# Rotary queries of latent attention: products formed from an SBUF copy made by ScalarE instead of from PSUM

## The chip, the cores and the metric

One Trainium2 chip, one core. The metric is the device time of one execution in microseconds. The five engines of the core run instruction streams of their own and meet at semaphores: TensorE (PE in the rows; PEld is its weight load), VectorE (DVE), ScalarE (ACT), GpSimd (POOL) and SyncE (SP), which issues most of the DMA.

## The reference, cut to what matters

Two decoder layers, one with multi-head latent attention (16 heads) and one with sliding-window attention, for a prompt of 1024 tokens and 8 sample tokens. The change is in the first. For every head:

```
q = einsum('bsc,chd->bshd', cq, w_qb)
q_nope, q_rope = q[..., :QK_NOPE], q[..., QK_NOPE:]
rot = concatenate([-xf[..., half:], xf[..., :half]])
q_rope = xf * cos + rot * sin
sc = (einsum(q_nope, k_nope) + einsum(q_rope, kpe)) * MLA_SCALE
o  = softmax(masked sc) @ v
```

The rotary part of a query has 64 rows, so two heads share one tile of 128 partitions.

## The kernel before, in words

The program has a phase that projects the inputs, a phase with the 16 heads (about 300 to 935 us of the span), and later phases that the diff does not touch. The heads phase is `mla_heads`. It is written out by hand: `tensor`, `vector`, `scalar`, `gpsimd` and `sync` each list, for an even and for an odd head, the order of their steps, and a step waits on semaphores for its inputs and its buffers. An engine never passes a step that waits.

Steps of TensorE. `job(kind, x, c)` projects keys (`k`, line 886, two jobs a head), queries (`qn`, line 880, three jobs of 344 columns), values (`v`, line 893) or the rotary queries of two heads (`qr`, line 880, three jobs in an even head: column chunks 2, 0 and 1, in this order). `score(h, t)` (lines 910 to 916) makes the scores of query tile t, `turn` (line 930) transposes probabilities, `mix` (line 946) multiplies them with the values. After the first twelve jobs all jobs use PSUM bank 7, one after the other: a job waits in `bank_read` until the job before it has been read. For a `qr` job this is `qr_mul`, five products.

The rotary chain of one `qr` job: `rope_products` on VectorE forms one product with the cosines over 128 partitions (line 769) and four with the sines over 32 partitions each (line 772), all from PSUM into `rot`; `rope_sum` (line 778) adds them; `high` on ScalarE rounds them into `qr` for each of the two heads (line 671); `rope_low` on VectorE writes the remainders (line 788) and raises `qr_lo`. `rot` has one buffer. `score(h, t)` waits for `qr_lo` of the column chunks that hold its tile: chunk 2 for tiles 6 and 7, chunk 0 for tiles 0 and 1, chunk 1 for tiles 3 to 5.

Other steps named below: `greatest` (line 797, VectorE, maximum of a tile's scores), `exponents` (line 698, ScalarE, waits for that maximum), `invert` (line 806), `norm` (line 607, GpSimd), `turned_high` and `turned_low` (lines 707 and 811), `apply_gate` (line 822), `low` of a k or qn job (lines 751 and 746), `cut` (lines 618 and 620, GpSimd, then two DMA issues) and `split` (lines 597 and 599, GpSimd, weights into a high and a low part).

The order around the third rotary job, in `even(h)` of TensorE and of VectorE:

```
job("qr", p, 1), mix(h, 1, 0), mix(h, 1, 1), job("k", h + 2, 0), score(h + 1, 1)      # then odd: turn, turn, score(h + 1, 4)
rope_products(p, 1), apply_gate(h, 1), rope_sum(p, 1), rope_low(p, 1), low("k", h + 2, 0)
```

Of the kernel before, what the change touches and what calls it, by code (L numbers as in the profile page):

```python
# [18 lines left out]
P = 128  # L19
# [5 lines left out]
CH = TOK // 3  # L25
# [17 lines left out]
ACT = mybir.ActivationFunctionType  # L43
ALU = mybir.AluOpType
# [403 lines left out]
def head_jobs():  # L448

    jobs = [("k", 0, 0), ("k", 0, 1), ("qn", 0, 2), ("qr", -1, 2), ("qn", 0, 0), ("qr", -1, 0), ("qn", 0, 1), ("qr", -1, 1)]  # L450
    jobs += [("v", 0, c) for c in range(4)]
    first = len(jobs)
    for h in range(H - 1):
        if h % 2 == 0:
            p = h // 2
            jobs += [j for j in (("k", h + 1, 0), ("k", h + 1, 1), ("qn", h + 1, 2), ("qr", p, 2), ("qr", p, 0),
                                 ("qn", h + 1, 0), ("qn", h + 1, 1), ("qr", p, 1), ("k", h + 2, 0)) if j[0] != "k" or j[1] < H]
        else:
            p = (h + 1) // 2
            jobs += [("k", h + 1, 1), ("qn", h + 1, 2), ("v", p, 0), ("qn", h + 1, 0), ("v", p, 1), ("v", p, 2),  # L460
                     ("qn", h + 1, 1), ("v", p, 3)]
    return jobs, first


JOBS, N_FIRST = head_jobs()
JOB_NO = {j: n for n, j in enumerate(JOBS)}
# [3 lines left out]
TURNED_NO = {j: n for n, j in enumerate(TURNED)}  # L470
# [19 lines left out]
def turned_heads(p):  # L490

    return [(e, 2 * p + 1 + e) for e in range(2) if 0 <= 2 * p + 1 + e < H]


def job_bank(n):

    return 7 - n % 4 if n < N_FIRST else 7
# [9 lines left out]
def mla_heads(nc, a, g, st):  # L507


    ps = g.ps  # L510
    def sb(name, shape, dt=F32):
        return st.enter_context(nc.sbuf_tensor(name, shape, dt))

    def sem(name):
        return st.enter_context(nc.semaphore(name))
# [4 lines left out]
    vh, vl = sb("b_vh", [P, 3, SEQ], R32), sb("b_vl", [P, 3, SEQ], R32)  # L520
    qh, ql = sb("b_qh", [P, 2, TOK], R32), sb("b_ql", [P, 2, TOK], R32)
    qr = sb("b_qr", [P, 3, TOK], R32)
    rot = sb("b_rot", [P, 2, CH])
    gate = sb("b_gate", [P, 4, 2 * P])
    prob = sb("b_prob", [P, 4, SEQ])
    pth, ptl = sb("b_pth", [P, 4, 512], R32), sb("b_ptl", [P, 4, 512], R32)
# [6 lines left out]
    w_rounded, w_split = sem("b_w_rounded"), sem("b_w_split")  # L533
    gate_in = [sem(f"b_gate_in{u}") for u in range(4)]
    pj_done, pj_hi, pj_lo = sem("b_pj_done"), sem("b_pj_hi"), sem("b_pj_lo")
    qr_mul, qr_rot, qr_hi, qr_lo, kept = sem("b_qr_mul"), sem("b_qr_rot"), sem("b_qr_hi"), sem("b_qr_lo"), g.qs_rope_kept
    scored, maxed, exped, inverted, normed = (sem("b_scored"), sem("b_maxed"), sem("b_exped"),
                                              sem("b_inverted"), sem("b_normed"))
    turned, pt_hi, pt_lo = sem("b_turned"), sem("b_pt_hi"), sem("b_pt_lo")
# [117 lines left out]
    def scalar(act):  # L657
        act.wait_ge(mask_in, 16)
        nc.scalar.activation(maskr[:], mask[:], ACT.Copy).then_inc(mask_ok, 1)

        def high(kind, x, c):

            if (kind, x, c) not in JOB_NO:
                return
            n = JOB_NO[(kind, x, c)]
            bank, cols = job_bank(n), slice(c * CH, (c + 1) * CH)
            if kind == "qr":
                act.wait_ge(qr_rot, TURNED_NO[(kind, x, c)] + 1)
                for e, h in turned_heads(x):
                    rows = qr_rows(e)[0]  # L670
                    nc.scalar.activation(qr[rows, h % 3, cols], rot[rows, 0, :], ACT.Copy, scale=MLA_SCALE).then_inc(qr_hi, 1)
                    if c == 2:
                        nc.scalar.activation(g.qs_rope[:, h, :], rot[rows, 0, CH - DEC:CH], ACT.Copy,
                                             scale=MLA_SCALE).then_inc(kept, 1)
                return
            act.wait_ge(pj_done, n + 1)
            if kind == "qn":
                if c == 2:
                    nc.scalar.activation(g.qs_nope[:, x, :], ps[:, bank, CH - DEC:CH], ACT.Copy,
                                         scale=MLA_SCALE).then_inc(g.qs_kept, 1)  # L680
                nc.scalar.activation(qh[:, x % 2, cols], ps[:, bank, 0:CH], ACT.Copy, scale=MLA_SCALE).then_inc(pj_hi, 1)
            elif kind == "k":
                nc.scalar.activation(kh[:, x % 2, c * 512:(c + 1) * 512], ps[:, bank, :], ACT.Copy).then_inc(pj_hi, 1)
            else:
                for i, (heads, slots) in enumerate(v_slots(x)):
                    copy = nc.scalar.activation(v_view(vh, slots, c), v_psum(bank, heads), ACT.Copy)
                copy.then_inc(pj_hi, 1)

        def exponents(h, t):
            if h >= H:  # L690
                return
            n, keys = tile_no(h, t), (t + 1) * P
            act.wait_ge(maxed, n + 1)
            if n >= 4:
                last = (h, t) if t is None else divmod(n - 4, NT)
                m = TILE_ORDER[last[1]] // 2
                act.wait_ge(turned, chunk_no(last[0], m, m) + 1)
            nc.scalar.activation(prob[:, n % 4, 0:keys],  # L698
                                 ps[:, 2 * (n % 2):2 * (n % 2) + 2, :].rearrange("p b n -> p (b n)")[:, 0:keys],
                                 ACT.Exp, bias=least[:, n % 4:n % 4 + 1], accum_out=total[:, n % 4:n % 4 + 1]).then_inc(exped, 1)  # L700

        def turned_high(h, m, c):
            n, cols = chunk_no(h, m, c), 512 if c < m else 384
            act.wait_ge(turned, n + 1)
            if due(n - 3):
                act.wait_ge(mixed, n - 3)
            nc.scalar.activation(pth[:, n % 4, 0:cols], ps[:, 4 + n % 2, 0:cols], ACT.Copy).then_inc(pt_hi, 1)  # L707

        def even(h):
            p = h // 2  # L710
            turned_high(h, 3, 0), turned_high(h, 3, 1), exponents(h, 1)
            high("k", h + 1, 0), turned_high(h, 3, 2), high("k", h + 1, 1)
            exponents(h, 4), exponents(h, 5)
            high("qn", h + 1, 2), turned_high(h, 3, 3), turned_high(h, 0, 0), turned_high(h, 2, 0)
            high("qr", p, 2), exponents(h, 2), exponents(h, 3)
            turned_high(h, 2, 1), turned_high(h, 2, 2)
            high("qr", p, 0), high("qn", h + 1, 0)
            exponents(h + 1, 6), turned_high(h, 1, 0), exponents(h + 1, 7)
            high("qn", h + 1, 1), turned_high(h, 1, 1), exponents(h + 1, 0)
            high("qr", p, 1), high("k", h + 2, 0)  # L720

        def odd(h):
            p = (h + 1) // 2
            turned_high(h, 3, 0), turned_high(h, 3, 1), exponents(h, 1)
            high("k", h + 1, 1), turned_high(h, 3, 2), high("qn", h + 1, 2), turned_high(h, 3, 3)
            exponents(h, 4), exponents(h, 5)
            high("v", p, 0), turned_high(h, 0, 0), exponents(h, 2), high("qn", h + 1, 0)
            turned_high(h, 2, 0), turned_high(h, 2, 1), high("v", p, 1), exponents(h, 3), high("v", p, 2)
            turned_high(h, 2, 2), exponents(h + 1, 6), turned_high(h, 1, 0), exponents(h + 1, 7)
            high("qn", h + 1, 1), turned_high(h, 1, 1), exponents(h + 1, 0), high("v", p, 3)  # L730

        for j in JOBS[:N_FIRST]:
            high(*j)
        exponents(0, 6), exponents(0, 7), exponents(0, 0)
        for h in range(0, H, 2):
            even(h), odd(h + 1)

    def vector(dve):
# [20 lines left out]
        def rope_products(p, c):  # L759
            if ("qr", p, c) not in JOB_NO:  # L760
                return
            n, k = JOB_NO[("qr", p, c)], TURNED_NO[("qr", p, c)]
            bank, cols = job_bank(n), slice(c * CH, (c + 1) * CH)
            dve.wait_ge(pj_done, n + 1)
            if k:
                dve.wait_ge(qr_hi, qr_halves[k - 1])
                dve.wait_ge(qr_lo, qr_halves[k - 1])
                dve.wait_ge(kept, sum(len(turned_heads(j[1])) for j in TURNED[:k] if j[2] == 2))
            nc.vector.tensor_tensor(rot[:, 0, :], ps[:, bank, 0:CH], g.cos[:, cols], ALU.mult).then_inc(qr_mul, 1)
            for r in range(4):  # L770
                to, src = slice(32 * r, 32 * r + 32), slice(32 * (r ^ 1), 32 * (r ^ 1) + 32)
                nc.vector.tensor_tensor(rot[to, 1, :], ps[src, bank, 0:CH], g.sin[src, cols], ALU.mult).then_inc(qr_mul, 1)

        def rope_sum(p, c):
            if ("qr", p, c) not in JOB_NO:
# [81 lines left out]
    def tensor(pe):  # L857
        def bank_read(n):

            if JOBS[n] in PLAIN_NO:  # L860
                pe.wait_ge(pj_lo, PLAIN_NO[JOBS[n]] + 1)
            else:
                pe.wait_ge(qr_mul, 5 * (TURNED_NO[JOBS[n]] + 1))

        def job(kind, x, c):

# [124 lines left out]
    p = Programs(sync, gpsimd, scalar, vector, tensor)  # L991
# [1724 lines left out]
```

## Time and profile before

| | |
|---|---|
| median of 3 runs | 1764.34 us (1761.11 to 1766.4) |
| profiled execution, its own time | 1767.28 us |
| its span | 1765.6 us |
| mean granted clock of TensorE | 0.961 |
| busy: TensorE, weight loads | 1630.6 us (92%), 1524.4 us (86%) |
| busy: VectorE, ScalarE, GpSimd | 827.7 us (47%), 545.1 us (31%), 740.0 us (42%) |

Shares are of the whole span. The view of waits adds up, for a waiting line, the idle time that one releasing line ended. The timelines give each instruction's start from the beginning of the span, its duration and, in brackets, the idle time of its engine before it where there was some. An "xN" merges N instructions in a row. "Issue" is an idle time for which the view found no releaser.

### The profile page before, as it was taken

The page shows a single profiled execution, that of the slowest core. Times are in us where ns is not written, and L with a number is a line of the kernel's source. Part 1 is how long each engine was busy: PE and PEld are TensorE (multiplying, and loading weights), DVE is VectorE, ACT ScalarE, POOL GpSimd, SP SyncE. Part 2 cuts the span into 40 slices and gives each one's busy share as a digit, 9 for nine tenths or more (in the row PEclk, how much of TensorE's full clock was granted, in tenths as well). Part 3 has the DMA queues.
Part 4 walks back from the last instruction along what each step waited for, and adds up shares of the span by engine and source line. Part 5 has one row for each costly group of instructions (what it writes and reads, how often), then busy time and mean ns, then how long its engine had stood idle before and what let it go on. Part 6 is the DMA issues. An engine that isn't in the chain of part 4 may idle for free. (4 is left out here: it accounts for less than half of the span.)

```text
span 1765.6 us, 28128 instructions
## 1 busy us (share of the span) xinstructions
PE 1630.6 (92%) x10778; PEld 1524.4 (86%) x10778; DVE 827.7 (47%) x1471; ACT 545.1 (31%) x1201; POOL 740.0 (42%) x894
## 2 busy tenths in 40 slices
PE   6999997899999999999997879998999999799797
PEld 6989997799999999998985569997899999576797
DVE  5127311576675756757563320029644210687016
ACT  5022111344444444444432210012322301575012
POOL 2323332255554555555445204546324222487410
PEclk9999998999999999999999998998999999799698
DMA  4112231111221112112149882252453212542214
GB/s 170 60 48 95 95 113 61 39 61 51 64 67 52 58 61 65 56 56 72 37 147 303 302 307 77 69 199 100 144 191 131 67 72 107 166 116 67 85 45 160
DMA packets 101406, 186.92 MB, mean 106 GB/s; under 512 B 11058, under 2 KB 65091, under 8 KB 100995
## 3 DMA queue, kind: packets, MB, share of 16 engines
q1 hardware_dynamic: 86628, 139.36, 23.7%
q0 software_dynamic: 8448, 24.65, 4.0%
q10 hardware_dynamic: 6208, 21.26, 3.0%
q8 instruction: 78, 1.28, 0.3%
q14 instruction: 44, 0.36, 0.1%
HBM read 137.42 MB, written 49.89 MB: 106 GB/s over the span
## 5 line engine op out<-in xcount | busy, mean ns | idle before, releaser
L607 POOL TENSOR_SCALAR b_prob<-b_prob,b_share 128x896 f32<-128x896 f32 (+7 forms) x128 | 97.1, 759 | 198.5 <-DVE b_share L806 196.7
L1649 POOL CAST w_hi_d<-w_raw_d 128x1024 fp32r<-128x1024 f32 x38 | 40.4, 1064 | 233.4 <-PE ps L129 128.5
L129 PE MATMUL ps<-a_xh,w_hi_a 128*128 128x344 f32 x552 | 119.6, 325 | 13.7 <-DVE a_xl L280 10.4
L707 ACT ACTIVATE b_pth<-ps 128x512 fp32r<-128x512 f32 (+1 forms) x160 | 86.2, 555 | 104.3 <-PE ps L930 94.7
L129 PE MATMUL ps<-a_xl,w_hi_a 128*128 128x344 f32 x552 | 118.1, 323 | 0.0
L129 PE MATMUL ps<-a_xh,w_lo_a 128*128 128x344 f32 x552 | 117.4, 321 | 0.0
L797 DVE TENSOR_REDUCE b_least<-ps 128x1 f32<-128x896 f32 (+7 forms) x128 | 96.3, 752 | 35.8 <-PE ps L916 35.1
L698 ACT ACTIVATE b_prob<-ps,b_least 128x896 f32<-128x896 f32 (+7 forms) x128 | 94.8, 743 | 57.3 <-DVE b_least L797 56.3
L811 DVE TENSOR_TENSOR b_ptl<-ps,b_pth 128x512 fp32r<-128x512 f32 (+1 forms) x160 | 99.2, 632 | 27.1 <-ACT b_pth L707 26.1
L129 PEld LDWEIGHTS ps<-a_xh,w_hi_a 128*128 128x128 f32 x552 | 93.8, 190 | 15.0 <-issue 10.8
L107 POOL CAST w_hi_a<-w_raw_a 128x1024 fp32r<-128x1024 f32 x23 | 24.9, 1082 | 181.6 <-PE ps L129 177.0
L880 PE MATMUL ps<-cqh,b_w_hi 128*128 128x344 f32 x300 | 99.2, 331 | 0.2 <-DVE b_ql L746 0.2
L880 PE MATMUL ps<-cql,b_w_hi 128*128 128x344 f32 x300 | 96.1, 320 | 0.0
L880 PE MATMUL ps<-cqh,b_w_lo 128*128 128x344 f32 x300 | 95.9, 320 | 0.0
L946 PE MATMUL ps<-b_pth,b_vh 128*128 128x256 f32 x320 | 93.1, 291 | 2.5 <-DVE b_ov L822 2.5
L129 PEld LDWEIGHTS ps<-a_xl,w_hi_a 128*128 128x128 f32 x552 | 94.5, 191 | 0.0
L930 PE MATMUL ps<-ident,b_prob 128*128 128x128 f32 x576 | 87.7, 278 | 5.7 <-POOL b_prob L607 5.5
L129 PEld LDWEIGHTS ps<-a_xh,w_lo_a 128*128 128x128 f32 x552 | 92.8, 189 | 0.0
L946 PE MATMUL ps<-b_pth,b_vl 128*128 128x256 f32 x320 | 90.1, 282 | 0.0
L946 PE MATMUL ps<-b_ptl,b_vh 128*128 128x256 f32 x320 | 89.9, 281 | 0.0
L1652 POOL TENSOR_TENSOR w_lo_d<-w_raw_d,w_hi_d 128x1024 fp32r<-128x1024 f32 x35 | 88.6, 2531 | 2.8
L1928 PE MATMUL ps<-xo_h,w_hi_d 128*128 128x344 f32 x304 | 81.9, 330 | 5.7 <-DVE w_lo_d L1800 3.6
(348 smaller groups left out, 4690.0 us busy)
## 6 DMA issues: line engine op xcount, KB each, us to landing
w_raw_d<-in_w_tiles SPq DMA_DIRECT2D x46, 512.0 KB, 3.6
c_pages<-in_cache_pages SPq DMA_DIRECT2D x80, 160.0 KB, 4.5
w_raw_a<-in_w_tiles SPq DMA_DIRECT2D x23, 512.0 KB, 3.5
gate_scratch<-a_stage ACTq DMA_DIRECT2D x16, 512.0 KB, 2.6
b_gate<-gate_scratch SPq DMA_DIRECT2D x64, 128.0 KB, 2.6
oh_scratch<-b_oh POOLq DMA_DIRECT2D x64, 128.0 KB, 2.1
ol_scratch<-b_ol POOLq DMA_DIRECT2D x64, 128.0 KB, 2.1
xo_h<-oh_scratch SPq DMA_DIRECT2D x16, 512.0 KB, 10.1
```

The lines of the kernel that those rows point to most:

```text
L129: mm = nc.tensor.matmul(ps[:, bank + c, 0:CH], wt, xt[:, k0 + k, c * CH:(c + 1) * CH], start=first and x == 0, stop=last and x == 2)
L607: nc.gpsimd.tensor_scalar(prob[:, n % 4, 0:keys], prob[:, n % 4, 0:keys], share[:, n % 4:n % 4 + 1], 1.0, ALU.mult, ALU.mult).then_inc(nor ...
L698: nc.scalar.activation(prob[:, n % 4, 0:keys], ps[:, 2 * (n % 2):2 * (n % 2) + 2, :].rearrange("p b n -> p (b n)")[:, 0:keys], ACT.Exp, bi ...
L707: nc.scalar.activation(pth[:, n % 4, 0:cols], ps[:, 4 + n % 2, 0:cols], ACT.Copy).then_inc(pt_hi, 1)
L797: nc.vector.tensor_reduce(least[:, n % 4:n % 4 + 1], ps[:, 2 * (n % 2):2 * (n % 2) + 2, :].rearrange("p b n -> p (b n)")[:, 0:keys], AX.X, ...
L811: nc.vector.tensor_tensor(ptl[:, n % 4, 0:cols], ps[:, 4 + n % 2, 0:cols], pth[:, n % 4, 0:cols].bitcast(F32), ALU.subtract).then_inc(pt_l ...
L880: mm = nc.tensor.matmul(ps[:, bank, 0:CH], wt[:, own], xt[:, k, c * CH:(c + 1) * CH], start=k == 0 and i == 0, stop=k == 3 and i == 2)
L930: mm = nc.tensor.transpose(ps[:, 4 + n % 2, col:col + P], prob[:, (first + q) % 4, (2 * c + b) * P:(2 * c + b + 1) * P], g.ident[:])
L946: mm = nc.tensor.matmul(ps[:, 6, 2 * P - wide:2 * P], vt[:, h % 3, v], pt[:, n % 4, col:col + wide], start=c == 0 and k == 0 and i == 0, s ...
L1649: nc.gpsimd.tensor_copy(hi, shaped(raw_tile(t), t)).then_inc(w.rounded, 1)
L1652: nc.gpsimd.tensor_tensor(lo, shaped(raw_tile(t), t), hi.bitcast(F32), ALU.subtract).then_inc(w.split, 1)
L1928: mm = nc.tensor.matmul(ps[:, bank + i, 0:CH], wt, xt[:, half * KT + k, c * CH:(c + 1) * CH], start=half == 0 and k == 0 and x == 0, stop= ...
```

## The change

ScalarE copies the bank of a `qr` job into a third slot of `rot` and raises `qr_raw`. The five products wait for that and read the copy. The bank is given to the next job when the copy is made. The copy waits until the products of the rotary job before it are done. In `even(h)` of ScalarE the copies stand at three places written by hand; in the first jobs each stands right before its `high`.

```diff
-    rot = sb("b_rot", [P, 2, CH])
+    rot = sb("b_rot", [P, 3, CH])
...
+        def raw_of(kind, p, c):
+            if (kind, p, c) not in JOB_NO:
+                return
+            n, k = JOB_NO[("qr", p, c)], TURNED_NO[("qr", p, c)]
+            act.wait_ge(pj_done, n + 1)
+            if k:
+                act.wait_ge(qr_mul, 5 * k)
+            nc.scalar.activation(rot[:, 2, :], ps[:, job_bank(n), 0:CH], ACT.Copy).then_inc(qr_raw, 1)
...
-            high("qn", h + 1, 2), turned_high(h, 3, 3), turned_high(h, 0, 0), turned_high(h, 2, 0)
-            high("qr", p, 2), exponents(h, 2), exponents(h, 3)
+            high("qn", h + 1, 2), turned_high(h, 3, 3), turned_high(h, 0, 0), raw_of("qr", p, 2), turned_high(h, 2, 0)
+            high("qr", p, 2), exponents(h, 2), exponents(h, 3), raw_of("qr", p, 0)
             turned_high(h, 2, 1), turned_high(h, 2, 2)
...
-            high("qr", p, 1), high("k", h + 2, 0)
+            raw_of("qr", p, 1), high("qr", p, 1), high("k", h + 2, 0)
...
         for j in JOBS[:N_FIRST]:
+            if j[0] == "qr":
+                raw_of(*j)
             high(*j)
...
-            dve.wait_ge(pj_done, n + 1)
+            dve.wait_ge(qr_raw, k + 1)
...
-            nc.vector.tensor_tensor(rot[:, 0, :], ps[:, bank, 0:CH], g.cos[:, cols], ALU.mult).then_inc(qr_mul, 1)
+            nc.vector.tensor_tensor(rot[:, 0, :], rot[:, 2, :], g.cos[:, cols], ALU.mult).then_inc(qr_mul, 1)
             for r in range(4):
                 to, src = slice(32 * r, 32 * r + 32), slice(32 * (r ^ 1), 32 * (r ^ 1) + 32)
-                nc.vector.tensor_tensor(rot[to, 1, :], ps[src, bank, 0:CH], g.sin[src, cols], ALU.mult).then_inc(qr_mul, 1)
+                nc.vector.tensor_tensor(rot[to, 1, :], rot[src, 2, :], g.sin[src, cols], ALU.mult).then_inc(qr_mul, 1)
...
-                pe.wait_ge(qr_mul, 5 * (TURNED_NO[JOBS[n]] + 1))
+                pe.wait_ge(qr_raw, TURNED_NO[JOBS[n]] + 1)
```

## Rows read from the trace of the kernel before

**Rows 1.** TensorE's waits, heads stage: line, releaser, us in total, times, longest.

```profile
PE ps L886 <- DVE b_rot L772: 10.7, 7, 1.5
...
PE ps L910 <- DVE b_vl L755: 2.8, 1, 2.8
PE ps L910 <- issue: 2.2, 1, 2.2
```

**Rows 2.** Timeline of TensorE around T in head 2: start, us, what, [idle before].

```profile
452.77 0.47 PE L886 MATMUL ps<-ckvh,b_w_hi 128*128 128x512 f32 x1 [1.52 <-DVE b_rot L772]
...
455.74 0.47 PE L910 MATMUL ps<-b_kh,b_qh 128*128 128x512 f32 x1
...
457.60 0.45 PE L886 MATMUL ps<-ckvh,b_w_hi 128*128 128x512 f32 x1
```

**Rows 3.** Timelines of VectorE, ScalarE and GpSimd at the same place.

```profile
449.94 0.52 DVE L769 TENSOR_TENSOR b_rot<-ps,cos 128x344 f32<-128x344 f32 x1 [1.45 <-PE ps L880]
450.49 2.14 DVE L772 TENSOR_TENSOR b_rot<-ps,sin 32x344 f32<-32x344 f32 x4
...
454.58 1.05 DVE L788 SCALAR_TENSOR_TENSOR b_qr<-b_rot,b_qr 64x344 fp32r<-64x344 f32 x2 [1.07 <-ACT b_qr L671]
...
453.54 1.01 ACT L671 ACTIVATE b_qr<-b_rot 64x344 fp32r<-64x344 f32 x2 [6.05 <-DVE b_rot L778]
...
450.12 0.73 POOL L620 TENSOR_TENSOR b_ol<-b_ov,b_oh 128x256 fp32r<-128x256 f32 x1
```

**Rows 4.** Timelines of TensorE, VectorE and GpSimd in the last even head.

```profile
912.64 0.62 PE L910 MATMUL ps<-b_kh,b_qh 128*128 128x512 f32 x1 [2.19 <-issue]
...
915.95 0.75 PE L930 MATMUL ps<-ident,b_prob 128*128 128x128 f32 x4
...
911.67 0.88 DVE L788 SCALAR_TENSOR_TENSOR b_qr<-b_rot,b_qr 64x344 fp32r<-64x344 f32 x1 [0.56 <-ACT b_qr L671]
...
907.00 0.73 POOL L620 TENSOR_TENSOR b_ol<-b_ov,b_oh 128x256 fp32r<-128x256 f32 x1
```

**Rows 5.** Groups of instructions by line: busy us, mean ns, idle before.

```profile
L681 ACT ACTIVATE b_qh<-ps 128x344 fp32r<-128x344 f32 x45 | 20.5, 456 | 12.0 <-PE ps L880 11.9
```

**Rows 6.** Instructions that write the rotary tile: ns minimum/median/maximum.

```profile
L772 DVE TENSOR_TENSOR b_rot<-ps,sin x108: 504/511/522, 310.7 to 909.7; 32x344 f32<-32x344 f32 x108
...
L788 DVE SCALAR_TENSOR_TENSOR b_qr<-b_rot,b_qr x48: 509/514/1512, 313.9 to 911.7; 64x344 fp32r<-64x344 f32 x48
...
L778 DVE TENSOR_TENSOR b_rot<-b_rot x27: 497/507/522, 312.9 to 910.6; 128x344 f32<-128x344 f32 x27
```

**Rows 7.** Timelines of VectorE, ScalarE, GpSimd, TensorE, middle of head 2.

```profile
427.82 0.52 DVE L769 TENSOR_TENSOR b_rot<-ps,cos 128x344 f32<-128x344 f32 x1 [0.75 <-PE ps L880]
...
432.82 1.48 DVE L788 SCALAR_TENSOR_TENSOR b_qr<-b_rot,b_qr 64x344 fp32r<-64x344 f32 x2 [0.37 <-ACT b_qr L671]
434.23 0.68 DVE L797 TENSOR_REDUCE b_least<-ps 128x1 f32<-128x512 f32 x1
...
435.02 0.50 DVE L769 TENSOR_TENSOR b_rot<-ps,cos 128x344 f32<-128x344 f32 x1
...
442.88 0.52 DVE L746 SCALAR_TENSOR_TENSOR b_ql<-ps,b_qh 128x344 fp32r<-128x344 f32 x1
...
434.94 0.69 ACT L698 ACTIVATE b_prob<-ps,b_least 128x512 f32<-128x512 f32 x1 [1.22 <-DVE b_least L797]
...
428.40 0.40 POOL L597 CAST b_w_hi<-b_w_raw 128x256 fp32r<-128x256 f32 x1
428.88 0.74 POOL L599 TENSOR_TENSOR b_w_lo<-b_w_raw,b_w_hi 128x256 fp32r<-128x256 f32 x1
...
433.00 0.94 POOL L620 TENSOR_TENSOR b_ol<-b_ov,b_oh 128x256 fp32r<-128x256 f32 x1
...
435.88 0.48 PE L910 MATMUL ps<-b_kh,b_qh 128*128 128x512 f32 x1
...
438.06 0.37 PE L880 MATMUL ps<-cqh,b_w_hi 128*128 128x344 f32 x1
...
443.54 0.23 PE L910 MATMUL ps<-b_kh,b_qh 128*128 128x128 f32 x1
```

**Rows 8.** Windows: us, busy of five engines, granted clock, DMA share, GB/s.

```profile
452.70:456.10 3.40, 3.33 (x22) 3.04 (x23) 2.26 (x5) 2.14 (x5) 2.44 (x4) 1.00 0.17 60
912.80:916.20 3.40, 3.40 (x13) 2.91 (x13) 1.48 (x5) 0.56 (x2) 1.24 (x3) 0.50 0.94 307
```

More of the change, by code:

```diff
@@ L535, in mla_heads @@
     pj_done, pj_hi, pj_lo = sem("b_pj_done"), sem("b_pj_hi"), sem("b_pj_lo")
-    qr_mul, qr_rot, qr_hi, qr_lo, kept = sem("b_qr_mul"), sem("b_qr_rot"), sem("b_qr_hi"), sem("b_qr_lo"), g.qs_rope_kept
+    qr_raw, qr_mul, qr_rot, qr_hi, qr_lo, kept = sem("b_qr_raw"), sem("b_qr_mul"), sem("b_qr_rot"), sem("b_qr_hi"), sem("b_qr_lo"), g.qs_rope_kept
     scored, maxed, exped, inverted, normed = (sem("b_scored"), sem("b_maxed"), sem("b_exped"),
@@ L761, in rope_products @@
                 return
-            n, k = JOB_NO[("qr", p, c)], TURNED_NO[("qr", p, c)]
-            bank, cols = job_bank(n), slice(c * CH, (c + 1) * CH)
-            dve.wait_ge(pj_done, n + 1)
+            k, cols = TURNED_NO[("qr", p, c)], slice(c * CH, (c + 1) * CH)
+            dve.wait_ge(qr_raw, k + 1)
             if k:
```

## Prediction

> **What bounds the kernel now.** I read the page first: TensorE is busy for 92% of the span, VectorE for 47%, ScalarE for 31%, GpSimd for 42%. So time goes up or down with what TensorE waits for. The view of waits over the heads stage, with TensorE as the waiting engine, shows what the diff can touch [rows 1]: seven waits of the k projection (L886) on the rotary products (L772), 10.7 us in all, and one wait of a score (L910) "on issue", 2.2 us.
>
> Both are one pattern, at the end of each even head. There TensorE runs the third rotary job (call its end T), two mixes, the next head's k job, a small score, two turns and the score of tile 4. All jobs share PSUM bank 7, so the k job waits until the five products have read it: TensorE idles 1.52 us before 452.77 [rows 2]. The products start at T = 449.94, the last ends at 452.63 [rows 3].
>
> The reader is to see a second edge. Score(h+1, 4) waits for `qr_lo` of this same job, which is raised by the last L788. That one ends at 454.58 + 1.05 = 455.63, and the score starts at 455.74, T + 5.80 [rows 2, 3]. Proof that it counts is the last even head, with no k job between: the mixes run straight into the small score and TensorE then idles 2.19 us, until 912.64, 0.09 us after L788 ends (911.67 + 0.88 = 912.55) [rows 4]. In the other seven heads the 1.52 us spent before the k job hide this edge. So removing the bank wait alone is worth nothing: TensorE would come to that score at 455.74 - 1.52 = 454.22 and wait 1.52 us there.
>
> The chain products, sum, ScalarE's high half, VectorE's low half is thus on TensorE's path, and the change makes it longer.
>
> **The change, part by part.**
>
> *Bank 7 free sooner.* It is released after one copy. A ScalarE copy of this size out of PSUM is 456 ns [rows 5]; ScalarE is idle at T, for 6.05 us before 453.54 [rows 3]. The bank is free at about T + 0.46, before the mixes end: the 7 x 1.52 = 10.7 us before the k jobs go, and by the edge above come back before score 4.
>
> *The copy in front of the products at T.* Products start 0.46 + 0.03 us later, the 0.03 being the step from ScalarE to VectorE (454.55 to 454.58 in [rows 3]): +0.49. The five products keep their price: L778, which already has two SBUF inputs at the full shape, has a median of 507 ns, the PSUM forms 511 [rows 6]. A gain is bounded by 135 x 10 ns, mostly hidden; I take 0.
>
> *GpSimd's side of it.* All five products now have two SBUF inputs. Such instructions collide with GpSimd in this trace: L788 has 509 ns at least and 1512 at most, while L772 (one SBUF, one PSUM input) stays within 504 to 522 [rows 6]. The pair of L788 at 432.82 takes 1.48 us instead of 1.05, and GpSimd's L620 beside it 0.94 instead of 0.73 [rows 7, 3]. Read closely: the second L788 ends at 434.30, so it really began at 433.79, 0.15 before L620's end at 433.94. The rule I read from these rows: the later one waits until 0.15 us before the earlier one's end. At T, L620 runs from 450.12 to 450.85 [rows 3]; the first product wants 450.43 and begins at about 450.70: +0.27. Together +0.76 on the chain at T; score 4 starts at 456.50 instead of 455.74. That is 7 x 0.76 = 5.3 us. In the last even head L620 ends at 907.74, before the copy would, and only +0.49 stays [rows 4].
>
> The Trainium skill says the same of the two sides (SBUF — State Buffer, Who interferes with whom): a VectorE instruction with two SBUF inputs contends with a GpSimd instruction that reads SBUF, and one with at most one SBUF input does not; it speaks against this change. By the opposite, that only L788's form collides, the sum below would be near 15 instead of 20.5. No row shows L772 with both inputs in SBUF.
>
> *The first rotary job (p, 2).* Copy: +0.49, products wanted at 428.31 instead of 427.82. GpSimd's L597 at 428.40 (0.40) and L599 at 428.88 (0.74) [rows 7] now slip in between products. By the reading above, L597 begins at 428.70 and ends at 429.10, product 2 begins at 428.95 rather than 428.85; L599 begins at 429.33 and ends at 430.07, product 3 at 429.92 rather than 429.49. So +0.10 + 0.43, and the chain is 1.02 us late. Nothing of TensorE waits for it yet: its `qr_lo` is needed at 435.88, where score(h+1, 6) starts, and L788 ends at 434.30 + 1.02 = 435.32 [rows 7]. But VectorE's queue behind it, greatest(h, 3) of 434.23 with it, is 1.02 us late.
>
> *The second rotary job (p, 0).* This is the largest term. The copy is queued on ScalarE behind exponents(h, 3), which waits for greatest(h, 3). That exponent starts at 434.94 [rows 7]; it will start at 435.96. It holds ScalarE for 0.69 us, the copy takes 0.46: products at 437.13, against 435.02 now [rows 7]: +2.11. Then VectorE has no idle from 435 until low(qn, h+1, 0) ends at 442.88 + 0.52 = 443.40, and score(h+1, 0) that waits for it starts at 443.54 [rows 7]. ScalarE's and GpSimd's steps in between hang on VectorE and shift with it. TensorE has some 0.08 us of slack: 2.11 - 0.08 = +2.03 per head, 7 heads, 14.2 us. Cover that does hold: the bank wait of qn(h+1, 0) ends with the copy at 437.1, the job begins at 438.06 [rows 7].
>
> *The last even head and the first jobs.* The last: +0.5 as above; its middle part is without a k or v split and has over a microsecond of room, 0. The first jobs: VectorE's chain starts one copy later and TensorE waits for its end (its b_vl) before the first score [rows 1]: +0.5. Bank waits of these jobs have four banks and cost 0.6 at most today.
>
> *What else is moved.* No DMA is added. ScalarE gets 27 x 0.46 = 12.4 us in a stage where it is idle half the time. `qr_mul` releases the sample stage's loads on SP; they move with the heads.
>
> *The clock.* After the 2.19 us gap TensorE's granted clock was 0.50 for 3.4 us; after the 1.52 us gap it was 1.00 [rows 8]. The slow stretch took 915.95 - 912.64 = 3.31 us for work that takes 457.60 - 455.74 = 1.86 at full clock: 1.45 us lost [rows 2, 4]. The new gaps are 456.50 - 454.22 = 2.28 us before score 4 and about 2.1 before score(h+1, 0), fourteen in all, close to the lower gap that was followed by a fall. Bounds: none falls, 0; all fall, 14 x 1.45 = 20.3 us. Nearest in length are the ones before score 4; I take 3 falls, 4.4 us.
>
> **Sum.** 14.2 + 5.3 + 0.5 + 0.5 + 4.4 = 24.9 us slower; 20.5 without the clock. Against the profiled execution's 1767.28 us that is 1792; that execution stands 2.9 above the median 1764.34 of the runs shown, so for a median I say 1789.
>
> **Rivals.**
> 1. *Faster.* If score 4 did not wait for the rope chain, the 10.7 us would be kept: 1764.3 - 10.7 = 1754. It decides from the point where the chain at T is less than 4.2 us long after T, and it is 5.7 now. Against it: the last even head's 2.19 us. It also needs the 14.2 us term to be hidden. 7%.
> 2. *Only the end of the head is late.* If VectorE finds room between 435 and 443 (its queue shows none) or the copy is not held by exponents(h, 3), the 14.2 goes and 5.3 + 1.0 stay: 1764.3 + 6.3 = 1771. 13%.
> 3. *The clock falls at nearly every new gap*: 20.5 + 20.3 = 40.8, 1805. For it: 2.19 fell. Against: the shorter ones are nearer to 1.52, where nothing fell. 10%.
> 4. *The change does not do what it says*, the bank coming free no sooner: the 1.52 gaps stay and the chain's 20.5 come beside some of them. ScalarE's queue is empty at T, so I give this no chance of its own.
>
> **How the numbers follow.** Forecast 70%. Its own range is 13 (no clash, no fall) to 34 us (eight falls): 1777 to 1798. The range for 8 in 10 takes in rival 2 and leaves out the faster case and the far end of rival 3: 1770 to 1800. About 0.3% (5.3 us) is what a measurement of this kernel can tell from no change: faster 0.07 (rival 1); within 0.3% 0.06, half of rival 2, whose 6.3 lies at that edge; slower 0.87.
>
> **What the profile of after would show.** Right: no wait of L886 on DVE; new waits of L910 before score(h+1, 4), about 2.3 us, seven times, and before score(h+1, 0), about 2 us; products (p, 0) starting some 1.2 us after the VectorE work in front of them; maxima of L769 and L772 well over 522 ns; a few more dips in PEclk between 350 and 930. Wrong: L910 waits of 1.5 us or less at score 4; products within 522 ns; the copy (p, 0) running before exponents(h, 3).

## The result, and the profile after

The changed kernel takes 1809.17 us (1806.43 to 1810.29, 4 runs) against 1765.37 us before: a ratio of 1.0245, interval 1.0227 to 1.0263. It is 43.8 us slower, where 24.9 us had been forecast and a range that ended at 1800.

The page of the changed kernel, TensorE's busy time and the 40 slices of its granted clock. The stage with the heads fills about slices 8 to 21.

```profile
PE 1651.1 (91%) x10778; PEld 1540.8 (85%) x10778; DVE 840.6 (47%) x1471; ACT 554.6 (31%) x1228; POOL 741.4 (41%) x894
...
PEclk9999998899999999999998998999989999799698
```

TensorE is busy for 20 us more with the same 10778 matmuls: it idles more, and it also runs slower. The view of its waits after the first jobs of the stage, of the changed kernel (the counterpart of [rows 1]; L896 is the former L886, L920 the former L910, L782 the former L772):

```profile
PE ps L920 <- issue: 16.8, 8, 2.7
PE ps L920 <- DVE b_ql L757: 12.5, 7, 1.8
```

No L896 row is left: the seven waits for the bank, 10.7 us, are gone. In their place the first score of the next head waits 12.5 us in seven heads, and the score of tile 4 waits 16.8 in eight. That is the pattern that was forecast. The timeline of TensorE in head 2 has both, the counterpart of [rows 2] and of the last of [rows 7]:

```profile
453.02 0.33 PE L920 MATMUL ps<-b_kh,b_qh 128*128 128x128 f32 x1 [1.81 <-DVE b_ql L757]
...
467.34 0.47 PE L920 MATMUL ps<-b_kh,b_qh 128*128 128x512 f32 x1 [1.98 <-issue]
```

The timelines of VectorE, ScalarE and GpSimd in the same head, the counterparts of [rows 3] and [rows 7]:

```profile
435.81 0.52 DVE L779 TENSOR_TENSOR b_rot<-b_rot,cos 128x344 f32<-128x344 f32 x1 [1.25 <-ACT b_rot L696]
436.36 2.64 DVE L782 TENSOR_TENSOR b_rot<-b_rot,sin 32x344 f32<-32x344 f32 x4
...
444.60 0.52 DVE L779 TENSOR_TENSOR b_rot<-b_rot,cos 128x344 f32<-128x344 f32 x1 [1.00 <-ACT b_rot L696]
...
452.45 0.52 DVE L757 SCALAR_TENSOR_TENSOR b_ql<-ps,b_qh 128x344 fp32r<-128x344 f32 x1
...
466.19 1.05 DVE L798 SCALAR_TENSOR_TENSOR b_qr<-b_rot,b_qr 64x344 fp32r<-64x344 f32 x2 [1.07 <-ACT b_qr L671]
...
443.44 0.69 ACT L707 ACTIVATE b_prob<-ps,b_least 128x512 f32<-128x512 f32 x1 [1.23 <-DVE b_least L807]
...
444.12 0.45 ACT L696 ACTIVATE b_rot<-ps 128x344 f32<-128x344 f32 x1
...
435.89 0.69 POOL L597 CAST b_w_hi<-b_w_raw 128x256 fp32r<-128x256 f32 x1
436.66 0.89 POOL L599 TENSOR_TENSOR b_w_lo<-b_w_raw,b_w_hi 128x256 fp32r<-128x256 f32 x1
```

Read them in order. The sine products of the first rotary job take 2.64 us for four instead of 2.14, and beside them GpSimd's L597 takes 0.69 instead of 0.40 and L599 0.89 instead of 0.74: each holds the other up. The second copy starts at 444.12, right behind the exponent of 443.44, and the products at 444.60 have waited 1.00 us for it. `low` of the qn job then ends at 452.97, and the score starts at 453.02. At the end of the head the last L798 ends at 467.24, and the score of tile 4 starts at 467.34.

What the forecast did not have in this size is the clock. Windows of the changed kernel behind these two starts, and over the heads (the counterpart of [rows 8]; the granted clock is the third number from the end):

```profile
454.60:458.00 3.40, 3.40 (x15) 3.34 (x15) 1.03 (x5) 1.71 (x5) 3.04 (x4) 0.50 0.17 59
468.00:471.40 3.40, 3.40 (x13) 2.89 (x12) 2.38 (x5) 0.56 (x2) 0.47 (x1) 0.53 0.11 39
...
345.00:940.00 595.00, 566.30 (x3709) 531.04 (x3708) 369.76 (x731) 250.45 (x588) 291.52 (x428) 0.97 0.17 54
```

TensorE ran at half its clock for about 3.4 us behind both waits. In the trace's record of the clock there are 13 such stretches from 345 us to 10 us behind the start of the last third job's products, and one in the kernel before. That one, and one of the 13, stand in the last even head; the other 12 are new and lie between the two milestones named below. The two waits of head 0 (1.55 and 2.27 us) are followed by none, so 12 of the 14 regular waits are.

One place in the stage's first jobs also came out far dearer than forecast. Timelines of VectorE and GpSimd there, in the changed kernel:

```profile
310.45 3.41 DVE L782 TENSOR_TENSOR b_rot<-b_rot,sin 32x344 f32<-32x344 f32 x4
...
316.51 3.55 DVE L782 TENSOR_TENSOR b_rot<-b_rot,sin 32x344 f32<-32x344 f32 x4
...
322.68 2.13 DVE L782 TENSOR_TENSOR b_rot<-b_rot,sin 32x344 f32<-32x344 f32 x4
...
310.97 1.43 POOL L599 TENSOR_TENSOR b_w_lo<-b_w_raw,b_w_hi 128x512 fp32r<-128x512 f32 x1
...
317.70 1.44 POOL L599 TENSOR_TENSOR b_w_lo<-b_w_raw,b_w_hi 128x512 fp32r<-128x512 f32 x1
```

Two of the three sets of sine products stand beside a weight split of GpSimd and take 3.4 to 3.6 us; the third stands alone and takes 2.13.

That is not all of the loss there. The first score starts 2.4 us later than before (329.38 instead of 326.97), the first turn 5.1 us later (340.71 instead of 335.65). Windows from the first score to the first turn, of the kernel before, of the changed kernel, and of two experiments of the next section, *third filled* (first jobs not copied) and *shorter chain* (first jobs copied):

```profile
326.97:335.65 8.68, 5.58 (x28) 4.62 (x28) 2.98 (x6) 2.76 (x6) 2.18 (x3) 1.00 0.00 0
```

```profile
329.38:340.71 11.33, 8.04 (x28) 6.80 (x28) 3.00 (x6) 2.76 (x6) 2.18 (x3) 0.75 0.00 0
```

```profile
327.57:339.01 11.44, 8.15 (x28) 6.88 (x28) 3.00 (x6) 2.76 (x6) 2.19 (x3) 0.74 0.00 0
```

```profile
330.62:339.34 8.72, 5.61 (x29) 4.63 (x29) 2.99 (x6) 2.97 (x7) 2.19 (x3) 1.00 0.00 0
```

The same work takes 8.7 us at full clock and 11.3 to 11.4 where the clock falls in it, and the fall comes without a copy in these jobs and stays away with one. So 2.4 us come from the copies and the collisions, and 2.7 from a fall of the clock that one profile each can't tie to the copies.

**Where the 43 us lie.** The third rotary job of each pair is a good milestone. Its first product starts, in heads 0 and 14, at these times (timelines of VectorE, kernel before, then changed kernel):

```profile
373.62 0.52 DVE L769 TENSOR_TENSOR b_rot<-ps,cos 128x344 f32<-128x344 f32 x1 [1.44 <-PE ps L880]
...
907.55 0.52 DVE L769 TENSOR_TENSOR b_rot<-ps,cos 128x344 f32<-128x344 f32 x1 [1.44 <-PE ps L880]
```

```profile
380.77 0.81 DVE L779 TENSOR_TENSOR b_rot<-b_rot,cos 128x344 f32<-128x344 f32 x1 [1.94 <-ACT b_rot L696]
...
950.26 0.52 DVE L779 TENSOR_TENSOR b_rot<-b_rot,cos 128x344 f32<-128x344 f32 x1 [1.94 <-ACT b_rot L696]
```

A pair of heads takes (907.55 - 373.62) / 7 = 76.28 us before and (950.26 - 380.77) / 7 = 81.36 after: 5.08 more, seven times, 35.6 us. Up to the first milestone another 7.2 are lost: the 5.1 above and one more wait of head 0. Behind the last one the changed kernel is 1.2 us shorter.

### The profile page after: what moved, and what is told of

Same layout as the page of the kernel before. It is cut to its first block and busy times, and to the rows that moved or that the text cites. A ratio compares the mean times of both kernels' runs of the same rounds, so it can differ in the third digit from the quotient of the medians.

```text
span 1807.1 us, 28181 instructions
## 1 busy us (share of the span) xinstructions
PE 1651.1 (91%) x10778; PEld 1540.8 (85%) x10778; DVE 840.6 (47%) x1471; ACT 554.6 (31%) x1228; POOL 741.4 (41%) x894
## 5 line engine op out<-in xcount | busy, mean ns | idle before, releaser
L920 PE MATMUL ps<-b_kh,b_qh 128*128 128x512 f32 (+1 forms) x192 | 72.7, 378 | 33.2 <-issue 16.8
L890 PE MATMUL ps<-cqh,b_w_lo 128*128 128x344 f32 x300 | 99.6, 332 | 0.0
```

What stands on the lines that cost most here:

```text
L890: mm = nc.tensor.matmul(ps[:, bank, 0:CH], wt[:, own], xt[:, k, c * CH:(c + 1) * CH], start=k == 0 and i == 0, stop=k == 3 and i == 2)
L920: nc.tensor.matmul(out, qh[:, h % 2, q], kh[:, h % 2, keys], start=True, stop=False)
```

## The experiments

A table of all first, with the pair of heads (from the same two milestones), the regular waits and the number of stretches at half clock (from 345 us to 10 us behind the last milestone). Medians are of all runs; the last three columns are of the one profiled execution of each kernel. Line numbers shift by a few lines from kernel to kernel; the tiles keep their names.

| kernel | median us | ratio to before (interval) | pair of heads us | waits in each pair us | half-clock stretches |
|---|---|---|---|---|---|
| before | 1764 to 1765 | 1 | 76.28 | 1.52 | 1 |
| changed | 1809.17 | 1.0245 (1.0227 to 1.0263) | 81.36 | 1.82, 1.98 | 13 |
| bank held | 1794.14 | 1.0140 (1.0102 to 1.0177) | 79.40 | 1.70, 2.28 | 3 |
| copy first | 1785.46 | 1.0107 (1.0075 to 1.0140) | 78.24 | 1.03, 2.28 | 1 |
| only third | 1782.62 | 1.0091 (1.0061 to 1.0121) | 78.47 | 2.27 | 7 |
| first from PSUM | 1803.01 | 1.0207 (1.0174 to 1.0241) | 81.31 | 1.82, 1.98 | 13 |
| copy, products from PSUM | 1782.85 | 1.0101 (1.0086 to 1.0115) | 78.47 | 1.19, 2.01 | 2 |
| filled | 1791.89 | 1.0156 (1.0141 to 1.0171) | 79.10 | 0.88 | 0 |
| third filled | 1771.39 | 1.0037 (1.0014 to 1.0060) | 77.14 | below 0.7 | 0 |
| shorter chain | 1789.02 | 1.0143 (1.0108 to 1.0178) | 78.70 | 1.48, 1.93 | 2 |
| only third, shorter chain | 1770.86 | 1.0031 (1.0014 to 1.0048) | 76.56 | 1.70 | 0 |
| reordered, copy | 1773.11 | 1.0044 (1.0031 to 1.0057) | 78.44 | 1.30 | 7 |
| reordered, no copy | 1779.20 | 1.0088 (1.0071 to 1.0106) | 77.97 | 2.13 | 6 |
| reordered, gate early | 1762.58 | 0.9991 (0.9975 to 1.0007) | 75.77 | 0.87 | 0 |

**Bank held: is the early bank worth anything?**

```diff
-                pe.wait_ge(qr_raw, TURNED_NO[JOBS[n]] + 1)
+                pe.wait_ge(qr_mul, 5 * (TURNED_NO[JOBS[n]] + 1))
```

> The changed kernel, but TensorE gets the bank back only when the five products are done, as before. Theory A (the early bank is worth nothing, because the score of tile 4 waits for the rotary chain anyway): the wait moves back to the k job, which then shows some 2.2 to 2.5 us, the wait before that score shrinks to about 0, and the time stays within 4 us of 1809. Rival (the early bank does save its 10.7 us in the changed kernel): 1820.

TensorE's waits with the bank held:

```profile
PE ps L896 <- DVE b_rot L782: 15.9, 7, 2.3
PE ps L890 <- DVE b_rot L782: 11.6, 7, 1.7
```

The wait before the k job is back at 2.28 us and the one before the score of tile 4 is gone from the list, as theory A had it; the other has moved from the score to the qn job in front of it. The early bank is worth nothing. But the time fell by 15 us, where theory A had it stay and the rival had it rise: the waits are as long as in the changed kernel, and the half-clock stretches fell from 13 to 3. At the 1.4 us a stretch that *filled* gives below, ten fewer are an estimated 14 of the 15 us. So in this kernel the early bank even loses: it moves the waits to places behind which the clock falls.

**Copy first: the queue behind the exponent.**

```diff
-            high("qr", p, 2), exponents(h, 2), exponents(h, 3), raw_of("qr", p, 0)
+            high("qr", p, 2), exponents(h, 2), raw_of("qr", p, 0), exponents(h, 3)
```

> The changed kernel with the copy of the second rotary job in front of exponents(h, 3) instead of behind it. Theory A (the queue behind the exponent is what makes VectorE late before score(h+1, 0)): that wait of 1.82 us falls to about 0.7 us and the clock does not fall after it: 7 x (1.1 + 1.6) = 19 us less, 1790. Rival (the collisions with GpSimd at the first rotary job make it late): the wait stays over 1.5 us and the time within 4 us of 1809.

Its waits, and the window over its heads:

```profile
PE ps L920 <- DVE b_ql L757: 7.2, 7, 1.1
```

```profile
345.00:920.00 575.00, 549.85 (x3720) 515.76 (x3719) 374.61 (x735) 252.88 (x594) 293.95 (x432) 1.00 0.17 56
```

The wait before score(h+1, 0) falls from 12.5 to 7.2 us in seven heads, 0.8 each. So the copy's place in ScalarE's queue was a real part of it. Most of the rest of the 24 us is the clock, which now stays up, behind the 2.28 us wait as well. The profiled execution is the fastest of its four (1780.62 us, the others 1784.51 to 1787.56), so the others may have a stretch or two more.

**Only third: one of the two places.** The copies of the other rotary jobs are left out; those products read PSUM and hold the bank as before.

```diff
+    def copied(p, c):
+        return p >= 0 and c == 1
...
-            dve.wait_ge(qr_raw, k + 1)
+            if copied(p, c):
+                dve.wait_ge(qr_raw, COPIES.index(("qr", p, c)) + 1)
+                source = rot[:, 2, :]
+            else:
+                dve.wait_ge(pj_done, JOB_NO[("qr", p, c)] + 1)
+                source = ps[:, job_bank(JOB_NO[("qr", p, c)]), 0:CH]
```

> Only the third rotary job of a pair is copied; first jobs, (p, 2) and (p, 0) are read from PSUM as before. Theory A: no wait before score(h+1, 0), and before score(h+1, 4) about 2 us instead of 1.5 before the k job: 7 x 0.46 = 3 us over before, and if a gap of about 2 us by itself makes the clock fall, 7 x 1.6 = 11 more: 1780. Rival (the clock falls only where both gaps stand in one head): 1769.

The product after the copy in head 2, a window over the heads, and GpSimd's instruction beside the product:

```profile
454.17 0.78 DVE L789 TENSOR_TENSOR b_rot<-b_rot,cos 128x344 f32<-128x344 f32 x1 [1.94 <-ACT b_rot L701]
```

```profile
345.00:940.00 595.00, 574.38 (x3842) 539.73 (x3841) 381.36 (x760) 254.05 (x593) 300.98 (x447) 0.98 0.19 61
```

```profile
453.85 0.73 POOL L625 TENSOR_TENSOR b_ol<-b_ov,b_oh 128x256 fp32r<-128x256 f32 x1
```

The product takes 0.78 us instead of 0.52 beside L625 (the former L620): the forecast's 0.27 us but for a hundredth. The wait is 2.27 us where the forecast had 2.28. And the same length that left the clock up with the copy first is followed by a half-clock stretch in six of the seven heads here. Head 8 is the exception: its wait, and windows behind it and behind that of head 10:

```profile
696.22 0.47 PE L933 MATMUL ps<-b_kh,b_qh 128*128 128x512 f32 x1 [2.27 <-issue]
```

```profile
696.20:699.60 3.40, 3.38 (x18) 2.88 (x19) 2.96 (x6) 1.00 (x3) 0.72 (x2) 1.00 0.23 77
774.40:777.80 3.40, 3.40 (x13) 2.92 (x12) 1.92 (x4) 0.43 (x2) 0.47 (x1) 0.50 0.01 4
```

**First from PSUM.** As the changed kernel, with `copied` true for `p >= 0`.

> The changed kernel, but the rotary jobs among the first twelve are read from PSUM. Theory A (their products with two SBUF inputs collide with GpSimd, which splits weights there without a pause, and cost 5.5 us up to the first turn): 5 to 6 us less, 1803.5. Rival (the loss there is made up later, or it is only a clock stretch that comes anyway): 1809.

6.2 us less, by theory A. The first turn comes at 335.76 instead of 340.71, as early as before. But the first milestone comes at 377.36 instead of 380.77, only 3.4 us earlier: here a half-clock stretch stands in head 0. And of the 5 us at the first turn 2.7 are a fall of the clock that *third filled* has without copies there. So the collisions are shown, at some 2.4 us with the copies, and that the total agrees with 5 to 6 is in part luck.

**Copy, products from PSUM: without a second SBUF input.** The products wait for the copy, which nobody reads, and take PSUM; the bank is held as in the first experiment.

```diff
-            nc.vector.tensor_tensor(rot[:, 0, :], rot[:, 2, :], g.cos[:, cols], ALU.mult).then_inc(qr_mul, 1)
+            nc.vector.tensor_tensor(rot[:, 0, :], ps[:, bank, 0:CH], g.cos[:, cols], ALU.mult).then_inc(qr_mul, 1)
```

(the four sine products likewise)

> The changed kernel, where the products wait for the copy but read PSUM, so that they have one SBUF input as before; the bank is held until they are done. Theory A (GpSimd's collisions are a smaller part): no product over 525 ns, the stage's first jobs 3 us shorter, the wait before score(h+1, 0) 0.3 to 0.5 us shorter; 4 to 7 us under the run with the bank held, more only where a fall of the clock goes too. Rival (collisions are most of the 44 us): within 10 us of 1765.

The view by tile, of this kernel and of the changed one (ns minimum, median, maximum):

```profile
L783 DVE TENSOR_TENSOR b_rot<-ps,sin x108: 504/512/522, 311.7 to 930.4; 32x344 f32<-32x344 f32 x108
```

```profile
L782 DVE TENSOR_TENSOR b_rot<-b_rot,sin x108: 504/510/1501, 310.5 to 952.4; 32x344 f32<-32x344 f32 x108
```

No product is over 522 ns any more, with the same shapes and numbers; the median is the same within 2 ns. That is the collision shown by itself: it comes with the second SBUF input. The run is 11.3 us under the one with the bank held, more than the 4 to 7 expected; the waits are 1.19 and 2.01 us instead of 1.70 and 2.28.

**Filled: the clock by itself.** Matmuls of 128 columns into the score's own bank, overwritten by the score, in the time in which TensorE would wait. They are extra work, not part of the computation.

```diff
+            fill = {4: 13, 0: 12}.get(t, 0) if h % 2 else 0
+            if fill:
+                pe.wait_ge(exped, n - 1)
+                for _ in range(fill):
+                    nc.tensor.matmul(ps[:, 2 * r, 0:P], g.identr[:], maskr[:], start=True, stop=True)
```

> The changed kernel with 12 and 13 matmuls of 128 columns, whose result is overwritten, in front of score(h+1, 0) and score(h+1, 4), in the time in which TensorE waits. Nothing else changes. Theory A (the clock's falls after the two gaps are a term of 20 us or more): no stretch at 0.5 after these scores, 14 x 1.6 = 22 us less, 1787. Rival (the falls lie beside other waits and cost nothing): 1809.

A window over the heads, a row of its waits, and the two milestones:

```profile
340.00:940.00 600.00, 586.78 (x4019) 552.80 (x4020) 382.64 (x756) 258.47 (x608) 302.10 (x445) 1.00 0.18 55
```

```profile
PE ps L915 <- ACT b_prob L707: 2.8, 7, 0.4
```

```profile
381.07 0.81 DVE L779 TENSOR_TENSOR b_rot<-b_rot,cos 128x344 f32<-128x344 f32 x1 [1.94 <-ACT b_rot L696]
...
934.78 0.52 DVE L779 TENSOR_TENSOR b_rot<-b_rot,cos 128x344 f32<-128x344 f32 x1 [1.94 <-ACT b_rot L696]
```

200 extra matmuls make the kernel 17.3 us faster. The clock is full throughout, and a pair of heads takes (934.78 - 381.07) / 7 = 79.10 us: 2.82 over before. So the change costs 2.8 us a pair without the clock, and 81.36 - 79.10 = 2.26 by the clock, 15.8 us for the 12 stretches between the milestones, 1.3 us each.

The last pair blurs this: there the 12 matmuls (1.45 us) stand before a score that has nothing to wait for. From the third job of head 2 to that of head 12 every pair of the changed kernel has two stretches. It takes (871.78 - 461.56) / 5 = 82.04 us, the filled kernel (856.23 - 460.34) / 5 = 79.18, the kernel before (831.25 - 449.94) / 5 = 76.26: 2.92 by waiting and 2.86 by the clock, 1.4 us a stretch.

**Third filled.** Only the third job copied, 15 such matmuls before the score of tile 4.

> The kernel that copies only the third rotary job, with 15 matmuls of 128 columns, whose result is overwritten, in front of score(h+1, 4), where it waits 2.27 us. Theory A (over before, 7 x 0.75 us of waiting, and the rest of its 17 us is slow clock after six of these waits): the falls go and the time is 1765.3 + 5.3 + at most 2 for matmuls that overrun, some 1771. Rival (the clock's stretches cost little and something else holds TensorE): 1780 or more.

1771.39 us, with 77.14 us a pair, 0.86 over before. The falls go, as theory A had it. Its ten runs lie between 1763.7 and 1778.81 us, so the agreement of the median with 1771 to half a microsecond is luck.

**Shorter chain.** The sum goes in front of the gate's product, and each low half waits for its own high half.

```diff
-            rope_products(p, 1), apply_gate(h, 1), rope_sum(p, 1), rope_low(p, 1), low("k", h + 2, 0)
+            rope_products(p, 1), rope_sum(p, 1), apply_gate(h, 1), rope_low(p, 1), low("k", h + 2, 0)
...
-            dve.wait_ge(qr_hi, qr_halves[k])
-            for e, h in turned_heads(p):
+            for i, (e, h) in enumerate(turned_heads(p)):
+                dve.wait_ge(qr_hi, qr_halves[k] - len(turned_heads(p)) + i + 1)
```

> The changed kernel with a shorter end of the rotary chain: the sum stands in front of the gate's product, and each half of L788's pair waits only for its own half from ScalarE. That is 0.34 + 0.49 us less between T and the score of tile 4. Theory A (TensorE waits there for this chain and nothing else): the wait of 1.98 us becomes 1.1 to 1.2, most falls of the clock after it go: 7 x 0.8 + up to 7 x 1.6 = 6 to 17 us less, 1792 to 1803. Rival (it waits for something else, the exponents or the transposes): the wait stays.

1789.02 us, under the expected band. The wait before the score of tile 4 stayed at 1.92 to 1.94 us in six heads instead of falling to 1.2, so on its face the rival's sign. A pair of heads is 2.66 us shorter all the same; 11 of 13 half-clock stretches are gone, an estimated 2 of the 2.66 us at 1.4 us a stretch. The trace shows why the wait stayed. In head 6, VectorE's first product and its last pair of the chain, and GpSimd beside that pair:

```profile
617.56 0.81 DVE L779 TENSOR_TENSOR b_rot<-b_rot,cos 128x344 f32<-128x344 f32 x1 [1.94 <-ACT b_rot L696]
...
621.70 1.49 DVE L798 SCALAR_TENSOR_TENSOR b_qr<-b_rot,b_qr 64x344 fp32r<-64x344 f32 x2 [0.29 <-ACT b_qr L671]
```

```profile
621.95 0.87 POOL L620 TENSOR_TENSOR b_ol<-b_ov,b_oh 128x256 fp32r<-128x256 f32 x1
```

The pair does start earlier, but now meets a GpSimd subtraction that it missed before: 1.49 us instead of 1.05. And the first product takes 0.81 us instead of 0.52. From 1.98 us, 0.83 less and 0.44 and 0.29 more make 1.88, against 1.93 measured. In head 2, where the product takes 0.52, the wait is 1.65. The pair ends at 623.19 and the score starts at 623.29. So TensorE does wait for the chain, and two collisions more took back most of the 0.83.

**Only third, shorter chain.**

> The same shorter end, with only the third rotary job copied. Theory A: the wait before score(h+1, 4) falls from 2.27 to about 1.45 us, no longer than the 1.52 of before, and the clock stays up: within 4 us of before, 1761 to 1768. Rival (falls depend on more than the length of the gap): some heads keep a stretch at 0.5, 1768 to 1776.

No stretch at half clock here, and the wait falls from 2.27 to 1.70 us, less than the 0.83 expected (the last pair takes 1.49 us here too) but plainly: TensorE does wait for this chain. 1770.86 us, ratio 1.0031: in the rival's band by time, though without its falls. The pairs are only 2.0 us over before; 3.4 more are lost up to the first milestone, where nothing is copied before head 0's third job and the clock again falls behind the first score.

**Reordered: hide the chain instead of shortening it.** The third rotary job runs before the last qn job of the head. With a copy, with PSUM, and with a copy, the gate's product right behind the first product and the shorter chain. The cut shows TensorE's order; VectorE's and ScalarE's steps are moved to match, and VectorE's products are taken in two or three groups.

```diff
-            job("qn", h + 1, 1), turn(h, 1, 1), mix(h, 2, 1), mix(h, 2, 2), job("qr", p, 1), mix(h, 1, 0), mix(h, 1, 1)
+            job("qr", p, 1), turn(h, 1, 1), mix(h, 2, 1), mix(h, 2, 2), job("qn", h + 1, 1), mix(h, 1, 0), mix(h, 1, 1)
```

> Only the third rotary job is copied, and it is run before the last qn job of the head instead of behind it, so that the whole chain has two more pieces of TensorE's work to hide behind. Theory A: no wait before the k job and none before score(h+1, 4): the 10.7 + 2.2 us of before go: 1753. Rival (the products there collide with GpSimd and push low(qn) out, and TensorE waits for that instead): 1765 or more.

Theory A missed. The two waits are gone, but TensorE waits 1.30 us for the gate's product, which stands behind products that GpSimd stretches (first product 0.97 us, two sine products 2.33), and half-clock stretches follow in all seven heads of the profiled execution. That one is the slowest of its five (1776.91 us at a mean clock of 0.957; the others 0.961 to 0.962), so the others probably have fewer.

> The same order without any copy: products from PSUM. The bank is then held for some 3.6 us (five products with a subtraction and a gate between them) behind a job that is followed by 1.7 us of other TensorE work. Theory A: a wait of about 2 us before the qn job in place of 1.52 before the k job, 1765 to 1780. Rival (the order alone is what helps): 1753.

As expected by A: a wait of 2.13 us for the bank before the qn job, 1779.20 us, six half-clock stretches for eight such waits.

> The third rotary job in front of the last qn job, copied, as in the earlier run with this order, but the gate's product and the turned chunk go before the four sine products, and the chain's end is shortened. Theory A: the wait of 1.3 us for the gate's product goes, none longer than 0.3 us takes its place, no falls: 1765.3 - 7 x 1.5 = 1755. Rival (GpSimd's instructions between the sine products make the chain late for low(qn) or for the score of tile 4): a wait of 0.5 to 1 us stays, 1760 to 1768.

TensorE's waits in this kernel, after the stage's first jobs:

```profile
PE ps L934 <- issue: 7.1, 8, 1.0
```

The score still waits 0.87 us for the chain. 0.5 us a pair is won, the clock stays up, and the kernel takes 1762.58 us, 0.9991 (0.9975 to 1.0007): no difference from before that can be told. The rival was nearer.

## Why the prediction was wrong, by its own steps

*The edge behind the bank wait: right.* The k job's wait went and came back before the score of tile 4, where it was looked for, and holding the bank again costs nothing (it even gains, by the clock).

*The copy in front of the products, +0.49: right.* In head 2 the copy of the second job takes 0.45 us and the products start 0.48 after it.

*GpSimd at T, +0.27: right as a rule, but in the changed kernel it occurs in one head and not in seven.* It shows in the kernel that copies only the third job (0.78 instead of 0.52) and in the changed kernel's head 0 (0.81). In heads 2 to 12 of the changed kernel the product takes 0.52 us:

```profile
461.56 0.52 DVE L779 TENSOR_TENSOR b_rot<-b_rot,cos 128x344 f32<-128x344 f32 x1 [1.94 <-ACT b_rot L696]
```

```profile
460.52 0.74 POOL L620 TENSOR_TENSOR b_ol<-b_ov,b_oh 128x256 fp32r<-128x256 f32 x1
```

The half-clock stretch in front of the third job makes that job late, and the subtraction is done 0.30 us before the product starts. That is why the wait is 1.98 us and not 2.28; with the clock up (bank held, copy first, filled) the product takes 0.77 to 0.82. In head 14 it is 0.52, as forecast there. The Trainium skill's rule on two SBUF inputs (SBUF — State Buffer, Who interferes with whom) agrees with the runs: 1501 ns at most with two, 522 with one.

*The first rotary job, +1.02: right in heads 2 to 12.* Five products take 439.00 - 435.81 = 3.19 us instead of 2.69, and 0.48 for the copy. In head 0 they take 2.68: no collision there.

*The second rotary job, +2.03 a head: right in mechanism, a little high.* The wait there is 1.82 us; with the copy moved in front of the exponent 1.03 remain.

*The last even head, +0.5: right.* Its wait before the score of tile 4 is 2.67 us instead of 2.19.

*The waiting terms together* were 2.03 + 0.76 = 2.79 us a pair. The filled kernel, where the clock is full and both collisions occur, has 2.92 in heads 2 to 12.

*The first jobs, +0.5: wrong.* The first score is 2.4 us late. The step counted the copy and forgot that the sine products there stand beside GpSimd's weight split: twice 1.3 to 1.4 us. The rule of the 0.15 us overlap had been applied to the pairs of heads only. Up to the first turn it is 5.1 us, with a fall of the clock for which the forecast had no term and whose link to the copies is not shown.

*The clock, +4.4: wrong, and the larger part of the miss.* This is the step that failed. The price of one stretch, 1.45 us, was right (1.4 measured in heads 2 to 12). The number was not: three falls behind fourteen new waits were taken, by the length of the waits alone, and 12 came, six behind waits of 1.98 us and six behind waits of 1.82. Their cost is 15.8 us and not 4.4. Rival 3 of the prediction, 1805, described what happened and got 10%.

The sum with these two terms as measured: 24.9 + (15.8 - 4.4) + (5.1 - 0.5) = 40.9, against 42.8 up to the last milestone and 43.8 between the medians. The forecast's own range does not follow from its terms either: without collisions and falls they give 14.9 us and not 13, and with eight falls 32.1 and not 34.

*What stays open* is what decides whether the clock falls behind a wait of this kind. Its length alone does not: 2.28 us was followed by no fall in the kernel with the copy first, 1.30 by seven in the first reordered one, and 2.27 by six in the one with only the third copy, where the same 2.27 us in head 8 was followed by none. In the changed kernel itself the longest of the regular waits, 2.27 us in head 0, was followed by none, and the 1.82 and 1.98 us of heads 2 to 12 by one each. No run here separates it.

## What to carry to other kernels

Before a wait on a buffer is removed, look for the next wait for the same producer: where the consumer needs the result of the chain a few microseconds later, an earlier buffer is worth nothing and a step put in front of the chain is paid for (0.49 us of copy and 0.27 of collision, 0.86 a pair in *third filled*). Shortening the chain need not give its length back: 0.83 us less moved VectorE into GpSimd's instructions, and 0.57 or less was gained. A copy that lets VectorE read SBUF gives its instructions a second SBUF input, and each of them can then wait for a GpSimd instruction: look at what GpSimd does at every place, the first jobs too. Where a change lengthens TensorE's regular waits to a couple of microseconds, price the clock as a term between nothing and all of them, and hold the range open to both; a few throwaway matmuls in the gap show what it is worth.

## What the runs showed of the hardware that was not expected

200 extra matmuls in TensorE's idle time took 17.3 us off the kernel (1809.17 to 1791.89), while the granted clock over the heads rose from 0.97 to 1.00. Waits of equal length, 2.27 and 2.28 us, were followed by half clock in six of seven heads of one kernel and in none of another. A fall of the clock also changed which instructions met: the product that takes 0.81 us beside GpSimd's subtraction at full clock takes 0.52 in the six heads in which a half-clock stretch came before it. And a set of four VectorE products of 32 partitions took 3.55 us instead of 2.13 beside one pair of GpSimd instructions of 2.05 us together: alternating with GpSimd, VectorE lost 1.4 us.
